# Eight unused columns in the table of small parameters, so that everything allocated behind it lies 32 bytes higher

## Time and profile before

| | |
|---|---|
| timed runs | 1207.05, 1209.46, 1209.95 us; median 1209.46 |
| the profiled execution | 1206.77 us, span 1205.0 us |
| TensorE busy | 1195.3 us (99%), 7641 matmuls |
| VectorE busy | 859.4 us (71%) |
| ScalarE busy | 644.1 us (53%) |
| POOL busy | 226.7 us (19%) |
| moved by DMA | 218.03 MB, 181 GB/s in the mean |

### The profile page before, as it was taken

One profiled execution on the slowest core, in us unless ns is written; L12 is line 12 of the kernel. 1 busy time (PEld: TensorE's weight loads), 2 busy tenths in 40 slices (PEclk: granted clock), 3 DMA queues, 4 the chain that ended last, 5 costly groups with the idle time before them and its releaser, 6 DMA issues.

```text
span 1205.0 us, 19183 instructions
## 1 busy us (share of the span) xinstructions
PE 1195.3 (99%) x7641; PEld 1059.0 (88%) x7641; DVE 859.4 (71%) x1178; ACT 644.1 (53%) x860; POOL 226.7 (19%) x115
## 2 busy tenths in 40 slices
PE   9999999999999999999999999999999999999997
PEld 6888888988899888888999988888899978888886
DVE  6877667788868877766788786655679777766353
ACT  6655444465655755544643455544446784554442
POOL 1443301000000234310000024520000240445001
PEclk9999999999999999999999999999999999999999
DMA  8555545953345554555545555555576304555550
GB/s 316 210 175 189 195 176 175 298 191 107 105 149 180 178 202 176 181 198 180 175 149 200 178 207 190 194 178 191 191 257 233 140 19 175 184 200 176 178 206 35
DMA packets 31567, 218.03 MB, mean 181 GB/s; under 512 B 3584, under 2 KB 3856, under 8 KB 6272
## 3 DMA queue, kind: packets, MB, share of 16 engines
q1 hardware_dynamic: 29712, 210.06, 49.5%
q0 software_dynamic: 1488, 6.05, 1.7%
q10 hardware_dynamic: 288, 0.79, 0.2%
HBM read 215.82 MB, written 4.22 MB: 183 GB/s over the span
## 4 chain that ended last, share of the span: by engine, by line
PE 98%; DVE 1%; DMA 1%; ACT 0%; POOL 0%; issue 0%; SPq 0%; DVEq 0%; ACTq 0%; POOLq 0%
PE bank L1634 38%; PE bank L1635 19%; PE bank L1627 8%; PE bank L1628 8%; PE bank L1629 8%; PE bank L1812 2%; PE bank L1813 2%; PE bank L1814 2%; PE bank L2069 1%; PE bank L1743 1%; PE bank L1745 1%; PE bank L1744 1%; PE bank L1841 1%; DMA raw<-weights 1%; PE bank L1963 0%; PE bank L1946 0%
## 5 line engine op out<-in xcount | busy, mean ns | idle before, releaser
L858 DVE TENSOR_TENSOR w_hl<-raw,w_hl 128x2048 fp32r<-128x2048 f32 x194 | 444.1, 2289 | 135.0 <-ACT w_hl L438 134.1
L438 ACT ACTIVATE w_hl<-raw 128x2048 fp32r<-128x2048 f32 x195 | 370.5, 1903 | 138.0 <-PE bank L1635 49.5
L1634 PE MATMUL bank<-x_hl,w_hl 128*128 128x512 f32 x908 | 321.9, 399 | 0.0
L377 POOL TENSOR_TENSOR hidden<-hid_f,hidden 128x256 fp32r<-128x256 f32 (+1 forms) x76 | 189.3, 2491 | 527.6 <-ACT hidden L521 311.0
L1635 PE MATMUL bank<-x_hl,w_hl 128*128 128x256 f32 x908 | 255.0, 281 | 0.0
L1634 PE MATMUL bank<-hidden,w_hl 128*128 128x512 f32 x608 | 215.0, 399 | 0.0
L1634 PEld LDWEIGHTS bank<-x_hl,w_hl 128*128 128x128 f32 x908 | 170.6, 188 | 42.5 <-issue 0.2
L1635 PEld LDWEIGHTS bank<-x_hl,w_hl 128*128 128x128 f32 x908 | 171.5, 189 | 0.1
L1635 PE MATMUL bank<-hidden,w_hl 128*128 128x256 f32 x608 | 170.8, 281 | 0.0
L1634 PE MATMUL bank<-y_hl,w_hl 128*128 128x512 f32 x448 | 159.0, 400 | 0.0
L499 ACT ACTIVATE second<-bank 128x512 f32<-128x512 f32 (+1 forms) x100 | 54.4, 544 | 185.6 <-PE bank L1635 185.6
(11 more groups left out here) (389 smaller groups left out, 1706.0 us busy)
## 6 DMA issues: line engine op xcount, KB each, us to landing
raw<-weights SPq DMA_DIRECT2D x197, 1024.0 KB, 4.9
bias_skew<-bias_rows POOLq DMA_DIRECT2D x1, 3072.0 KB, 25.1
gate_or_bias<-bias_skew POOLq DMA_DIRECT2D x1, 2048.0 KB, 10.4
h<-x_t SPq DMA_DIRECT2D x2, 512.0 KB, 5.6
con<-consts SPq DMA_DIRECT2D x1, 769.5 KB, 12.6
raw<-weights ACTq DMA_DIRECT2D x1, 512.0 KB, 5.2
raw<-weights SPq DMA_DIRECT2D x1, 512.0 KB, 7.2
sv<-last_gain POOLq DMA_DIRECT2D x1, 512.0 KB, 3.7
```

The source lines that it names most:

```text
L377: nc.gpsimd.tensor_tensor(hidden[:, at, 1, :], src, hidden[:, at, 0, :].bitcast(F32), ALU.subtract).then_inc(hid_lo, 1)
L438: nc.scalar.activation(dst, src, ACT.Copy).then_inc(hi_split, 1)
L858: V.tensor_tensor(w_lo[:, s, :], raw[:, s, :], w_hi[:, s, :].bitcast(F32), ALU.subtract).then_inc(lo_split, 1)
L1634: mm(out_, w_hi[:, s, c:c + m], x, start=start, stop=False, **kw)
```

## The change

A new entry of eight columns, `spare`, stands in the list of small parameters between the gains and the convolution weights. Nothing reads it, and the host leaves it at zero. `par` grows from 392 to 400 columns, or from 1568 to 1600 bytes per partition, and so does the tensor `small` in HBM from which it is loaded. The columns of `par` behind the new ones and all tensors allocated behind `par` lie 32 bytes higher. No instruction is added or taken away.

```diff
 _small = [("ffn1", 8), ("mix", 8), ("c_q", 3), ("c_kv", 2), ("ffn2", 8), ("ple", 8), ("mix0", 8),
-          ("mlp0", 8), ("kv", 8), ("mix1", 8), ("mlp1", 8), ("conv_w", 24),
+          ("mlp0", 8), ("kv", 8), ("mix1", 8), ("mlp1", 8), ("spare", 8), ("conv_w", 24),
           ("q_head", 1), ("k_head", 1), ("k_rot", 1), ("pe_k", 16), ("pe_v", 16), ("phi_k2", 128), ("phi_v2", 128)]
```

## The result

Four timed runs of the changed kernel lie between 1194.96 and 1198.21 us, with a median of 1196.96; four of the kernel before, taken beside them, have a median of 1208.56 (1207.05 to 1209.95). The ratio is 0.9903, 95% interval 0.9882 to 0.9924. The change makes the kernel **faster by 11.6 us, 1.0%**.

A forecast was written before the change was run, and what follows sets the result against it. The prediction took the issue of 7641 matmuls on TensorE, plus a start and a tail, to bound the kernel. All terms were 0, added to the median 1209.46, giving 1209.5 us, range 1205.9 to 1212.8.

The forecast's parts named there:

- The step that failed: Whole kernel: heavy tensors stay in place, so only readers of moved tensors were priced; total 0 us.
- Stationary reads: TensorE loading the moved constants or ones as matmul weights: a start 32 bytes further costs 0 us.
- Moving reads: TensorE streaming moved tensors as the moving operand: 0, bound 4 ns per matmul, -1.2 to +1.2 us in all.
- taps, gains and tail: Convolution taps, gain scaling and last small stat operations on the vector engines: 0, at most 0.05 us in the tail.
- The shift takes place: Allocator taken to round to 32 bytes, so tensors really move; with rounding to 64 they would stay, same forecast.
- The start and the longer load: First gains' DMA: 0, at most 0.45 us; parameter table's 4 KB more: 0.01 us, hidden, so 0.
- a landing earlier by any amount gives nothing: At the start, earlier gains save 0 us, since warm-up matmuls keep TensorE until 9.76 us.
- the rule on reads off a 256-byte boundary: Table load: at most one extra 256-byte transaction for each of 128 rows, 0.1 us, hidden.
- Slower moving reads: Rival: streamed constants, now 32 past a multiple of 64, halve the pace of 220 matmuls; 24 us slower, 1234 us; chance 0.04.
- The gap at 932 us: Rival: a split, DMA, split loop without slack; a slower weight load adds 6.4 us, 1215.9 us; chance 0.03.
- one sign of being wrong: Profile after: a wait of over 1 us before a TensorE line that had none would show the forecast wrong.
- Ones and zeros gain: Rival: moved to a multiple of 64, 36 products with the ones gain 0.19 us each, 7 us, 1202.6 us; chance 0.04.

The follow-up runs named there:

- the first two experiments: Kernel before with only the ones moved to a multiple of 64: 1199.24 us; changed kernel with its ones back at 32 past one: 1207.72 us.
- the second experiment: Changed kernel with only its ones put back at 32 bytes past a multiple of 64: 1207.72 us, ratio 1.0001 to the kernel before.
- the probe on `ident`: Changed kernel plus one unused 256-column matmul behind each network's fourth chunk, weights `ident` at 32 past a multiple of 64; no time in the text.

## Why the prediction was wrong

**The step that failed** is the one by which the cost was made up: "Everything heavy (raw, w_hl, h, x_hl, y_hl, hidden, heads, second, the temporaries) is allocated ahead of the table and stays", and from it a sum over the readers of the moved tensors alone. That takes the time of an instruction that doesn't move as fixed. It isn't: 1763 pairs that read nothing moved take 346.7 in place of 353.3 ns, 11.8 us, where the sum had no term and its bound was 1.2. Of these, 1740 go by the address of the ones, as the first two experiments show.

**Stationary reads, 0 ns:** right for the duration (190 ns for the load, 377/378/379 for the matmul), and the wrong thing to look at. What moved is the restart of the stream, by a few ns that vanish in a duration: 115 or 118 ns from load to matmul, 1136 or 1128 to the second L1635. Behind it up to 511 pairs take one pace or the other.

**Moving reads, 0 within 4 ns; taps, gains and tail, 0:** right by their rows above, and by the second experiment, where they are moved and the time stays within 0.15%. **The shift takes place:** right; without it nothing would have changed. **The start and the longer load:** right in size. The gains let ScalarE begin at 6.05 in place of 6.28 us, and the constants land in 12.7 in place of 12.6. That "a landing earlier by any amount gives nothing" was wrong, with no weight in the sum: the first real matmul came at 9.53 in place of 9.76 us. In both traces it began 0.83 us behind the start of VectorE's first split (8.93 and 8.70 us), so it probably waited for that and not for the warm-up matmuls, and the earlier gains brought it forward. The prediction's estimate from the rule on reads off a 256-byte boundary (the Trainium skill, DMA: Bandwidth & Descriptors, How a descriptor splits into AXI transactions) was at most 0.1 us for the new pitch. No run here can show it: the constants landed in 12.1 to 13.1 us in the traces with the old table and in 12.3 to 13.2 with the new one.

**The rivals.** Slower moving reads: no sign of it. The gap at 932 us did widen, by the mechanism named: a slower load (7.17 in place of 6.18 us) in a loop without slack cost 1.0 us. So one sign of being wrong came, a wait of over 1 us where there was none, but it has no part in the gain. Ones and zeros gain: the tensor and the sign are right, but by luck. It was priced as 0.19 us for each of 36 matmuls, 7 us, and they gained nothing; what gained stands behind four sums of squares, 8 of the 36.

**Could it be seen?** The trace of before has one pace only, so not its size. But it had a hint that I didn't read: pairs of identical shape went at distances of 361, 349 and 350 ns in turn. If an instruction's own work alone set the pace, they would be equal. It is a hint and no more, as the faster pace has unequal distances too (350 and 343).

## What to carry to other kernels

In a stream of matmuls, read the distances of their starts, not the durations, and take a repeating unequal pattern as a hint that the pace may be one of several. A matmul that breaks the stream, its width or an operand's start address can move all that follows by 2%; here one to two columns or 8 to 32 bytes did. So price an edit that "only" shifts a restart at both paces, and before crediting an edit with a gain of that size, look whether unchanged instructions took another pace.

## What of the hardware was unexpected

**Two steady paces for the same pairs.** A matmul of 512 and one of 256 columns, each with a load of 128 x 128 weights, go at 353.3 or at 346.7 ns in every run here, at a granted clock of 1.00. Once taken, a pace held over as many as 511 pairs, until a break. The faster one itself comes in two patterns of the same mean: 350 and 343 ns in the changed kernel, 347, 346 and 347 behind the probe on `ident` there.

**The start of an operand shows as 2 to 3 ns** between the load and its matmul: in the second network, ones at 32 past a multiple of 64 gave 115 ns, at 0 gave 118. This distance isn't enough to tell the pace: 8, 16 and 32 all gave 115 and two of them the fast pace.

**What stays open.** Why there are two paces, and what in the engine has a period of four columns, no row shows. That the ones' address acts through the phase of the restart is inferred: the address moves the restart by some ns, a column or two of width can change the pace with every start address held, and one program, in two executions on two chips, took either. A probe that keeps the byte at which its operand ends and varies only its time would test it; there is none here. Nor was it tried to take the runs of 48, 39 and 16 pairs, slow in every kernel, to the other pace. At 183 pairs that is 1.2 us at most.
